# Expert blocks of 64 rows in the first layer's mixture of experts: two experts share one 128-row tile

## The reference

```python
grp = jnp.argmax(pg, axis=-1)
top_logit, top_e = lax.top_k(el_grp, TOP_K)
gate = pg_top * jax.nn.softmax(top_logit, axis=-1)
expert = (grp[:, None] * EXPERTS_PER_GROUP + top_e).reshape(-1)
...
def expert_block(args):
    xb, e = args
    return (jax.nn.silu(xb @ w1[e]) * (xb @ w3[e])) @ w2[e]
```

## Time and profile before

| | |
|---|---|
| median of 3 runs | 3617.43 us (3616.87 to 3619.02) |
| the profiled execution's own time | 3630.23 us |
| its span | 3628.4 us |
| TensorE busy | 3256.2 us (90%) |
| VectorE, ScalarE busy | 1881.6 us (52%), 1318.6 us (36%) |
| mean granted TensorE clock | 0.934 |
| HBM read and written | 459.28 MB, 25.17 MB |

### The profile page before, as it was taken

How to read it: one execution, slowest core, us unless ns; L and a number is a source line. 1 busy time by engine, 2 the same in 40 slices (tenths; PEclk the granted TensorE clock), 3 DMA queues, 4 the chain that set the end, 5 groups by cost and what they waited for, 6 DMA issues and landing times.

```text
span 3628.4 us, 35675 instructions
## 1 busy us (share of the span) xinstructions
PE 3256.2 (90%) x14016; PEld 2396.1 (66%) x14016; DVE 1881.6 (52%) x2763; ACT 1318.6 (36%) x1957; POOL 44.4 (1%) x76
## 2 busy tenths in 40 slices
PE   7997988699999967899899899999799978869997
PEld 3644886567767634688665678877477756648785
DVE  5344754556656544423473345554498956433343
ACT  2215223455555433225244322223422255332333
POOL 0000000000000000000000000000000000000000
PEclk9997999799999988789899999999899989789998
DMA  8330001699999951112013225551021211032220
GB/s 296 137 119 1 1 1 64 238 374 386 389 375 388 382 206 61 70 70 93 24 48 108 72 73 184 185 178 64 24 99 70 93 47 47 1 116 93 93 70 23
DMA packets 146804, 486.33 MB, mean 134 GB/s; under 512 B 8176, under 2 KB 11888, under 8 KB 134128
## 3 DMA queue, kind: packets, MB, share of 16 engines
q1 hardware_dynamic: 130544, 438.58, 32.5%
q10 hardware_dynamic: 10368, 24.92, 1.8%
q0 software_dynamic: 5760, 20.97, 1.5%
HBM read 459.28 MB, written 25.17 MB: 134 GB/s over the span
## 4 chain that ended last, share of the span: by engine, by line
PE 82%; DVE 8%; ACT 4%; issue 3%; DMA 1%; SPq 0%; POOL 0%; POOLq 0%; ACTq 0%; DVEq 0%; PEldq 0%
PE bank L456 17%; PE bank L458 17%; PE bank L457 17%; PE bank L1663 5%; PE bank L355 5%; PE bank L2274 3%; PE bank L559 2%; PE bank L1147 2%; PE bank L2899 1%; PE bank L551 1%; PE bank L1631 1%; PE bank L2068 1%; PE bank L2067 1%; DMA ring<-in_w_ada 1%; PE bank L2937 1%
## 5 line engine op out<-in xcount | busy, mean ns | idle before, releaser
L457 PE MATMUL bank<-h_parts,A_parts 128*128 128x512 f32 x1424 | 560.6, 394 | 0.0
L445 ACT ACTIVATE A_parts<-ring 128x1024 fp32r<-128x1024 f32 x178 | 187.3, 1053 | 462.0 <-PE bank L458 461.2
L456 PE MATMUL bank<-h_parts,A_parts 128*128 128x512 f32 x816 | 322.7, 396 | 35.9 <-DVE h_parts L3184 13.4
L458 PE MATMUL bank<-h_parts,ring_parts 128*128 128x512 f32 x896 | 353.4, 394 | 0.0
L452 DVE TENSOR_TENSOR ring_parts<-ring,A_parts 128x1024 fp32r<-128x1024 f32 x178 | 217.5, 1223 | 250.9 <-ACT A_parts L445 250.9
L457 PEld LDWEIGHTS bank<-h_parts,A_parts 128*128 128x128 f32 x1424 | 271.7, 191 | 59.0 <-issue 3.8
L456 PE MATMUL bank<-A_parts 128*128 128x512 f32 x672 | 265.9, 396 | 8.6 <-DVE A_parts L2609 5.2
L1702 DVE TENSOR_TENSOR ring_parts<-ring,h_parts 128x1024 fp32r<-128x1024 f32 x192 | 225.7, 1220 | 41.8 <-ACT h_parts L1765 40.9
L458 PE MATMUL bank<-A_parts,ring_parts 128*128 128x512 f32 x624 | 245.9, 394 | 0.0
L458 PE MATMUL bank<-h_parts,A_parts 128*128 128x512 f32 x576 | 226.8, 394 | 0.0
L457 PE MATMUL bank<-ring_parts 128*128 128x512 f32 x544 | 214.8, 395 | 0.0
(11 more groups left out here) (512 smaller groups left out, 5768.3 us busy)
## 6 DMA issues: line engine op xcount, KB each, us to landing
ring<-in_expert_w SPq DMA_DIRECT2D x64, 2048.0 KB, 9.6
ring<-in_w_in SPq DMA_DIRECT2D x37, 2048.0 KB, 8.1
A<-in_expert_w SPq DMA_DIRECT2D x32, 2048.0 KB, 8.3
ring<-in_w_ada SPq DMA_DIRECT2D x24, 2048.0 KB, 12.5
ring<-in_w_ff SPq DMA_DIRECT2D x16, 2048.0 KB, 8.4
slot_rows<-A ACTq DMA_DIRECT2D x32, 512.0 KB, 9.6
ring<-in_w_ffn_gate SPq DMA_DIRECT2D x5, 2048.0 KB, 7.9
ring<-in_w_ffn_up SPq DMA_DIRECT2D x5, 2048.0 KB, 7.9
```

Source lines behind the costliest of these rows:

```text
L445: act.activation(parts(s.shaped(high(s.q % 2))), s.raw(), ACT.Copy).then_inc(sem("split_high"), 1)
L456: pe.matmul(out, parts(w_high), parts(r_low), start=start, stop=False)
L457: pe.matmul(out, parts(w_high), parts(r_high), start=False, stop=False)
L458: return pe.matmul(out, parts(w_low), parts(r_high), start=False, stop=stop)
```

## The change

A block has CAP = 64 rows. Two blocks, 2i and 2i + 1, lie in one tile of 128 rows, so there is one gather, one turn into PSUM banks 2 and 3, one row split, one copy of the result and one store for both. Up to 15 spill blocks are foreseen, and the pair count and tables reach further. The w1 and w3 products take 64 stationary columns each, those of their block. The hidden rows of block 0 are split (hid_high on ScalarE, hid_split on VectorE), and its w2 is the fifth matrix that is split in pieces (MOE_IN), numbered -1 in the next round; its down product is made of 24 fp32r passes into PSUM partitions 0 to 63. That of block 1 stays in plain fp32 (down_whole) and writes partitions 64 to 127 of the same banks. The order of TensorE, VectorE and ScalarE at the start of a round is new: TensorE turns the rows first, ScalarE copies them first and then splits w2. SP's order of loads is unchanged. The core of the diff:

```diff
@@ -34,8 +34,10 @@
 GH, GD, GC = 4, 128, 64
 GN = T // GC
 N_EXP, D_EXP, EPG, N_GRP = 32, 512, 8, 4
-N_SPILL = (2 * T - N_EXP) // P
+CAP = 64
+N_SPILL = (2 * T - N_EXP) // CAP
 N_BLK = N_EXP + N_SPILL + 1
+N_PAIR = N_BLK // 2
 
...
             pe.wait_ge(*seen("route_place", 1))
-            for i in range(2 * TT):
-                mm = pe.matmul(bank[5][:, 0:N_BLK], on_rem(i), on_blk(i), start=(i == 0), stop=(i == 2 * TT - 1))
+            for s in range(2):
+                for i in range(2 * TT):
+                    mm = pe.matmul(bank[5][CAP * s:CAP * (s + 1), 0:N_PAIR], on_rem(i), on_blk(i)[:, s:N_BLK:2],
+                                   start=(i == 0), stop=(i == 2 * TT - 1))
...
-            step(dve.tensor_scalar(n_spill, cnt, float(P), None, ALU.is_gt))
-            for j in range(2, TT):
-                step(dve.scalar_tensor_tensor(n_spill, cnt, float(P * j), n_spill, ALU.is_gt, ALU.add))
+            step(dve.tensor_scalar(n_spill, cnt, float(CAP), None, ALU.is_gt))
+            for j in range(2, T // CAP):
+                step(dve.scalar_tensor_tensor(n_spill, cnt, float(CAP * j), n_spill, ALU.is_gt, ALU.add))
...
-            step(dve.tensor_scalar(quot, rank, float(P), None, ALU.is_ge))
+            step(dve.tensor_scalar(quot, rank, float(CAP), None, ALU.is_ge))
             step(dve.tensor_copy(over, quot))
-            for j in range(2, TT):
-                step(dve.scalar_tensor_tensor(quot, rank, float(P * j), quot, ALU.is_ge, ALU.add))
-            step(dve.scalar_tensor_tensor(rem, quot, -float(P), rank, ALU.mult, ALU.add))
+            for j in range(2, T // CAP):
+                step(dve.scalar_tensor_tensor(quot, rank, float(CAP * j), quot, ALU.is_ge, ALU.add))
+            step(dve.scalar_tensor_tensor(rem, quot, -float(CAP), rank, ALU.mult, ALU.add))
...
-            dve.tensor_tensor(rem_all, spread(iota, 2 * TT), spread(rem, P, at=2), ALU.is_equal)
+            dve.tensor_tensor(rem_all, spread(iota[:, 0:CAP], 2 * TT), spread(rem, CAP, at=2), ALU.is_equal)
...
+            for c in (0, 8):
+                step(dve.tensor_tensor(e32(prod), spread(iota[:, c:c + 8], 32, at=2), spread(spill_end, 8), ALU.is_ge))
+                step(dve.tensor_reduce(table_f[:, 32 + c:40 + c], e32(prod), AX_X, ALU.add))
...
+            step(dve.tensor_scalar(n_pairs, iota[:, 0:8], 2.0, None, ALU.mult))
...
+        rows_in = A[:, 16:18, :].rearrange("p a n -> p (a n)")
+        rows_high = A[:, 20:22, :].rearrange("p a n -> p (a n)")
+        rows_low = A[:, 22:24, :].rearrange("p a n -> p (a n)")
+        rows_out = A[:, 28:30, :].rearrange("p a n -> p (a n)")
+        HALF = (slice(0, CAP), slice(CAP, P))
+        hid = lambda s: W(24 + s)[0:CAP, :]
+        gate_act = lambda s: W(26 + s)[0:CAP, :]
+        hid_t = lambda s: W(41 + s)[:, 0:4 * CAP]
+        hid_low = W(43)[:, 0:4 * CAP]
+        MOE_IN = ((0, 0), (0, 1), (1, 0), (1, 1), (0, 2))
+        N_IN = len(MOE_IN)
...
-            for b in range(N_EXP, N_BLK):
+            for b in range(N_EXP * CAP // P, N_BLK * CAP // P):
...
+                pool.wait_ge(sem("moe_rows_free"), i + 1)
+                pool.tensor_copy(slot_cur[:, 0:1], slot_tok[:, bass.ds(i, 1)]).then_inc(sem("moe_idx"), 1)
+
+                pool.wait_ge(sem("moe_idx"), i + 1)
+                pool.sem_inc(sem("moe_gathers"), 1)
+                pool.indirect_dma_start(rows_in, None, tok_rows, bass.IndirectOffsetOnAxis(ap=slot_cur[:, 0:1], axis=0))\
+                    .then_inc(sem("moe_rows"), 16)
 
...
+            def rows_turn(i):
+
+                pe.wait_ge(sem("moe_rows"), 16 * i + 16)
                 for k in range(KD):
-                    mm = pe.transpose(bank[4 + 2 * s + k // 4][:, (k % 4) * P:(k % 4 + 1) * P],
-                                      rows_in(s)[:, k:D:KD], sq("ident"))
+                    mm = pe.transpose(bank[2 + k // 4][:, (k % 4) * P:(k % 4 + 1) * P], rows_in[:, k:D:KD], sq("ident"))
...
+                        c, n = slice(k * P + CAP * s, k * P + CAP * (s + 1)), slice((k % 2) * T, (k % 2 + 1) * T)
+                        mm = three_passes(pe, bank[4 + 2 * s + j][0:CAP, :], rows_high[:, c], rows_low[:, c],
...
+            def down(i, pieces=range(4)):
+
+                for f in pieces:
+                    if f == 0:
+                        pe.wait_ge(sem("moe_hid_t"), 2 * i + 1)
+                        pe.wait_ge(sem("moe_y_read"), i)
+                    pe.wait_ge(sem("moe_low"), 4 * N_IN * i + (f + 1))
+                    c = slice(f * CAP, (f + 1) * CAP)
+                    for h_ in range(2):
+                        n = slice(h_ * T, (h_ + 1) * T)
+                        mm = three_passes(pe, bank[h_][HALF[0], :], hid_t(0)[:, c], hid_low[:, c],
+                                          moe_high(f)[:, n], moe_raw(4, f)[:, n], f == 0, f == 3)
+                    mm.then_inc(sem("moe_downed" if f == 3 else "moe_used"), 1)
+
+            def down_whole(i):
+
+                pe.wait_ge(sem("moe_hid_t"), 2 * i + 2)
+                pe.wait_ge(sem("moe_w21"), 16 * i)
+                wt = moe_w(1, 2).rearrange("p (f n) -> p f n", f=4)
+                for h_ in range(2):
+                    for f in range(4):
+                        mm = pe.matmul(bank[h_][HALF[1], :], hid_t(1)[:, f * CAP:(f + 1) * CAP],
+                                       wt[:, f, h_ * T:(h_ + 1) * T], start=(f == 0), stop=(f == 3))
+                mm.then_inc(sem("moe_downed"), 1)
 
...
                 gated(i, 0)
-                rows_turn(i, 1)
                 gated(i, 1)
                 gated(i, 2, (0, 1))
                 hid_turn(i, 0)
                 gated(i, 2, (2, 3))
                 gated(i, 3)
 
-            rows_turn(0, 0)
+            rows_turn(0)
             inward(0)
             with pe.Fori(1, n) as i:
-                down(i, 0, 0)
+                rows_turn(i)
+                down(i, (0, 1))
                 hid_turn(i, 1, 2)
-                down(i, 0, 1)
-                rows_turn(i, 0)
-                down(i, 1, 0)
-                down(i, 1, 1)
+                down(i, (2, 3))
+                down_whole(i)
                 inward(i)
-            down(n, 0, 0)
+            down(n, (0, 1))
             hid_turn(n, 1, 2)
-            down(n, 0, 1)
-            down(n, 1, 0)
-            down(n, 1, 1)
+            down(n, (2, 3))
+            down_whole(n)
 
...
+            def outward(i):
+
+                gate(i, 1, 2)
+                low(i, -1, (0, 1))
+                hid_copy(i)
+                low(i, -1, (2, 3))
 
             def inward(i):
-                rows_split(i, 0)
+                rows_split(i)
                 low(i, 0)
-                low(i, 1, (0, 1, 2))
-                rows_split(i, 1)
-                low(i, 1, (3,))
-                low(i, 2, (0, 1, 2))
+                low(i, 1)
+                low(i, 2, (0, 1))
                 gate(i, 0)
-                low(i, 2, (3,))
-                low(i, 3, (0,))
-                hid_copy(i, 0)
-                low(i, 3, (1, 2, 3))
+                low(i, 2, (2, 3))
+                hid_split(i)
+                low(i, 3)
 
             inward(0)
             with dve.Fori(1, n) as i:
-                gate(i, 1, 2)
-                hid_copy(i, 1, 2)
+                outward(i)
                 inward(i)
-            gate(n, 1, 2)
-            hid_copy(n, 1, 2)
+            outward(n)
 
...
+            def rows_copy(i):
+
+                act.wait_ge(sem("moe_rows_free"), i + 2)
                 for c in range(2):
-                    ins = act.activation(parts(rows_high(s)[:, c * T:(c + 1) * T]), bank[4 + 2 * s + c][:], ACT.Copy)
...
+            def hid_high(i):
+                act.wait_ge(sem("moe_hid_turned"), 2 * i + 3)
+                act.activation(parts(hid_t(0)), bank[4][:, 0:4 * CAP], ACT.Copy).then_inc(sem("moe_hid_high"), 1)
+
+            def y_copy(i):
+
+                act.wait_ge(sem("moe_downed"), 2 * i + 2)
+                act.wait_ge(sem("moe_out"), 16 * i)
                 for c in range(2):
...
+            def y_out(i):
+                act.wait_ge(sem("moe_y_read"), i + 2)
+                act.dma_start(out_v[bass.ds(i - 1, 1), :, :].rearrange("b p n -> (b p) n"), rows_out)\
+                    .then_inc(sem("moe_out"), 16)
...
             def inward(i):
-                high(i, 1, (0, 1, 2))
-                rows_copy(i, 1)
-                high(i, 1, (3,))
+                high(i, 1)
                 silu(i, 0)
                 high(i, 2)
+                hid_high(i)
                 high(i, 3)
                 silu(i, 1)
 
-            rows_copy(0, 0)
+            rows_copy(0)
             high(0, 0, fresh=True)
             inward(0)
             with act.Fori(1, n) as i:
-                y_copy(i, 0)
-                rows_copy(i, 0)
-                y_out(i, 0)
+                rows_copy(i)
+                high(i, -1)
                 high(i, 0)
-                y_copy(i, 1)
-                y_out(i, 1)
```

(54 more changed lines are left out.)

105 lines of the change are left out of this document (34 added, 71 removed).

## The result

The change makes the kernel 5.7% slower: 3824.89 us (median of 4 runs, 3822.43 to 3828.35) against 3617.62 (4 runs, 3616.87 to 3619.02), a ratio of 1.0566 with an interval of 1.0551 to 1.0581. The forecast was 3735 (3.3% slower), its range ended at 3784. The profiled execution took 3828.35 us with a span of 3826.5.

A forecast was written before the change was run, and what follows sets the result against it. TensorE's instructions were taken to set the round, 38.32 us a pair. 17 rounds of 40.5 us against 15 of 38.32, plus 1 us for ends and 3 for routing, made +118 us: 3735 us, range 3692 to 3784.

The forecast's parts named there:

- Part one: Expert stage: four half-size blocks spill, so the pair count goes from 16 to 18, bounds 16 and 18.
- Part two: TensorE's work in a pair, one piece after the other: 36.1 us, with a pass at 0.228 us.
- Part three: New TensorE stops of 3.6 us before the first down product and 1.8 us within it: 41.5 us a pair.
- Part four: Array halves: the second down product's 6.87 us lies beside the gated passes, so a pair takes 38.1 us, not 41.5.
- Part five: TensorE clock: stops bring the half clock, adding 2.4 us a pair (from 0 to 4), giving 40.5 us.
- Rival 1: Array halves do not overlap where it counts: 42.8 us a pair, +157, 3774 us; chance 0.33.
- Rivals 2 to 4: Full clock, 3694 us, chance 0.12; seventeen pairs, 3695 us, 0.05; sixteen pairs, 3600 us or no change, 0.04.
- rival 2: Expert stage: the clock stays up, with the overlap, 38.1 us a pair, +77, 3694 us; chance 0.12.
- rival 4: Expert stage: no expert over 64, so 16 pairs, each needing under 38.1 us; 3600 us or no change; chance 0.04.

The follow-up runs named there:

- the kernel with the halves in turn: Changed kernel with both down products in plain fp32, all matmuls of one half ahead of the other's: 3683.79 us, ratio 1.0172.
- the kernel without stops: Changed kernel with w2 split before the copy of turned rows, its subtractions ahead of gate and hidden copy: 3682.92 us, ratio 1.0172.

## Why the prediction was wrong

**Part one, the count, was right**: 18 stores, 108 loads, and leaving out two pairs takes 93 us off the span.

**Part two, TensorE's work, was nearly right**: 36.1 us forecast, 37.2 with the stops cured. The missing 1.1 us: passes with 64 stationary columns come 0.231 apart rather than 0.228 (so the lower bound of 0.215 was no use), a hidden turn takes 0.62 to 0.64 where the earlier trace rows has 0.47, the second down product 7.01 for 6.87, and the first pass after an fp32 group or a turn takes 0.37 to 0.38 in place of 0.23.

**Part three, the stops, was right** in place, cause and size: 3.38 for 3.6 and 1.65 for 1.8, released by the subtraction, which waits for the split behind the copy of the rows.

**Part four is the step that failed.** "So matmuls on different halves do run beside each other" was read from the earlier trace rows and carried over to the second down product beside the gated passes. The scan's two groups are of one kind, fp32; these are fp32 and fp32r. The changed kernel's timeline shows no fp32r pass beside the 7.30 us of the fp32 group, and the experiment with alternating matmuls shows none either, while two fp32 products do overlap, completely. The step failed in a second way as well: it took a whole block of sixteen records to be hidden, and the kernel with the halves in turn shows that even fp32 beside fp32 gains only 14.0 (twice 7.01) less 12.26, some 1.8 us, in block order. The scan row, whose two groups stand one behind the other in the program as well, had said no more: the prediction's own 3.6 less the 2.88 measured is 0.7 us, three to four records of 0.213, and not the eight that a full overlap hides. The Trainium skill (TensorEngine Tiling (Array Packing), Key Properties) lets different tiles run in parallel and makes no condition on types there. The runs agree for fp32 alone. The Trainium skill's rule that matmuls start in program order (TensorE: Matmul & The Clock Gate, Part 3) is not kept by the last timeline: a record of the second half begins at 911.30, ahead of three records of the first, 911.72 to 912.58, that stand before it in the program. What withholds the overlap between the kinds, a mode of the whole array or something in the queue, is open. Two fp32r products on different halves weren't tried, so whether the mixture or fp32r itself stands in the way is open too. Part four also has a slip: it starts the second down product at 10.8 us of the round, and part three ends it at 18.9, which means a start at 12.0. Nothing in the sum hangs on it.

**Part five, the clock, had its sign and not its size.** 2.4 us a round were put in and 3.2 measured. The priced case was one stop of 3.10 us with the half clock behind it, at 1.6; in the round shown both stops are followed by the half clock, the one of 1.65 us too, and more than eight passes are slowed: between 956.58 and 961.27, and again from 964.91 until the fp32 group, which takes 7.30 in place of 7.0.

**Rival 1 is the case that came**, with chance 0.33 and a price of 42.8 us a pair. That price was 2.9 short: 1.1 of TensorE's work and 1.9 of the clock (1.3 forecast, 3.2 measured), less 0.4 for stops that were forecast too long, and 0.3 that the sum of the parts leaves unexplained. 17 x 2.9 = 49 us are why the time lies 41 us above the range's end. The range took in the rival's centre, 3774, with hardly any room for an error in its terms. Rivals 2 to 4 were not seen; the kernel without stops comes near rival 2's sum (3683 and 3694), by other terms. Even at full clock and with no stops the changed kernel is slower, by rival 4's own reckoning: it decides at the count, and once there are eighteen pairs, one has to take less than 15/17 of before's, 33.8 us.

## What to carry to other kernels

Two independent products can share TensorE's time when each fills half of the columns, both are plain fp32, and their matmuls alternate in the program: look in a trace for pairs of records that begin together, and do not carry the overlap over to another type or order. In each helper engine's list, work that needs only loaded data belongs ahead of work that waits for the engine being fed: reordering two such lists was worth 142 us here. Halving a block saves only what a row count governs, so count the blocks it adds first.

## What the runs showed of the hardware

- Two fp32 products with 64 stationary columns each overlap wholly when alternated (32 records in 7.09 us), and by four of sixteen records at the border when one follows the other (12.26 us). fp32 with fp32r does not overlap at all, in block order or in alternation, and some 0.15 us are lost at each change of kind (1.84 us where the sum is 1.55).
- After a stop of 1.65 us the clock falls to half in three rounds of four, at a cost of 1.5 to 1.6 us, and in others of the same run it does not. Two stops a round cost more clock (3.2 to 3.5 us) than the two alone together (1.1 and 1.5). Transposes of a constant in the stops kept the clock at 1.00.
- The core's transfers ran at 423 GB/s for 500 us; the stage before showed 374 to 389, which therefore was no ceiling.
